# Hybrid decoder layer on one core: the routing stage works by sets of tiles with three-slot rings, and one raw buffer stays allocated across three stages

## The reference

```
mod = silu(c) @ w_ada + b_ada;  sh1, sc1, g1, sh2, sc2, g2 = split(mod, 6)
u   = x * (1 + sc1) + sh1
proj = u @ w_in                      # conv B | conv C | conv x | q | k | v | gate_A | gate_B
y_a = (B * dwconv3(C * xc)) @ w_a;   y_b = stick_breaking_attention(q, k, v) @ w_b
mix = (sigmoid(gA) * y_a + sigmoid(gB) * y_b) @ w_o
x   = layer_norm(alpha * x + g1 * mix)
u2  = x * (1 + sc2) + sh2
aff = sigmoid(u2 @ w_router)         # 16 experts in 4 groups
# best group by the sum of its top 2 of (aff + b_router), top 2 experts in it,
# gates = their aff over the sum; a token's row goes to both experts, in blocks of 128 rows
ffn = sum over both of gate * (silu(u2 @ w_gate[e]) * (u2 @ w_up[e])) @ w_down[e]
out = layer_norm(alpha * x + g2 * ffn)
```

## Time and profile before

| | us |
|---|---|
| median of three runs | 2847.39 (2843.78 to 2850.57) |
| the profiled execution | 2846.57 |
| its span, first to last instruction | 2844.0 |
| PE busy | 2526.8 (89%) |
| DVE busy | 1517.7 (53%) |
| ACT busy | 1118.3 (39%) |
| POOL busy | 866.5 (30%) |
| mean granted PE clock | 0.940 |
| one high part of 128x1024 on ACT (L1270) | 1.06 |
| one copy-out of u2, two halves, on ACT (L1285) | 1.08 |
| one sum of two products of a unit on POOL (L1060) | 1.28 |
| one turn of a tile's u2 on PE up to the next instruction (L1238) | 0.87 |

### The profile page before, as it was taken

How to read it: one execution, slowest core, us unless ns; L and a number is a source line. 1 busy time by engine, 2 the same in 40 slices (tenths; PEclk the granted TensorE clock), 3 DMA queues, 4 the chain that set the end, 5 groups by cost and what they waited for, 6 DMA issues and landing times. The chain is left out here.

```text
span 2844.0 us, 37196 instructions
## 1 busy us (share of the span) xinstructions
PE 2526.8 (89%) x12564; PEld 2105.7 (74%) x12565; DVE 1517.7 (53%) x2156; ACT 1118.3 (39%) x1817; POOL 866.5 (30%) x755
## 2 busy tenths in 40 slices
PE   4999799899999999999969969993998999999970
PEld 3888677778888888888857747883787888888750
DVE  4211165666565666566632248985556544526636
ACT  2211154554454545454520012220556545536633
POOL 1111044442222222222301225664222222322236
PEclk7999899999999999999989989995999999999985
DMA  6655687767666575646455554343667656636735
GB/s 236 246 188 184 187 266 223 233 211 221 200 202 195 196 219 167 205 153 200 147 193 168 160 189 134 126 133 113 210 192 228 205 149 180 204 91 198 259 74 236
DMA packets 252442, 534.86 MB, mean 188 GB/s; under 512 B 23156, under 2 KB 92904, under 8 KB 250664
## 3 DMA queue, kind: packets, MB, share of 16 engines
q1 hardware_dynamic: 229736, 468.39, 50.1%
q0 software_dynamic: 15248, 46.62, 7.7%
q10 hardware_dynamic: 7344, 18.35, 1.7%
HBM read 380.26 MB, written 153.02 MB: 188 GB/s over the span
## 5 line engine op out<-in xcount | busy, mean ns | idle before, releaser
L89 PE MATMUL mx_acc<-u_u,mx_w_hi 128*128 128x512 f32 x1792 | 572.7, 401 | 2.1 <-DMA mx_w_lo<-halves 2.1
L608 POOL TENSOR_TENSOR mx_wt<-mx_wt,mx_rest 128x127 f32<-128x127 f32 (+15 forms) x128 | 271.4, 2120 | 701.1 <-DVE mx_rest L813 701.1
L89 PEld LDWEIGHTS mx_acc<-u_u,mx_w_hi 128*128 128x128 f32 x1792 | 326.8, 190 | 66.5 <-DMA mx_w_lo<-halves 2.5
L821 DVE TENSOR_TENSOR mx_wt_lo<-mx_p_t,mx_wt_hi 128x512 fp32r<-128x512 f32 (+2 forms) x320 | 192.1, 604 | 332.5 <-ACT mx_wt_hi L774 330.4
L89 PE MATMUL mx_acc<-u_u,mx_w_lo 128*128 128x512 f32 x896 | 354.2, 395 | 0.0
L774 ACT ACTIVATE mx_wt_hi<-mx_p_t 128x512 fp32r<-128x512 f32 (+2 forms) x320 | 170.5, 533 | 400.4 <-PE mx_p_t L662 353.5
L813 DVE TENSOR_TENSOR_SCAN mx_rest<-mx_rest,mx_zero 128x128 f32<-128x128 f32 (+15 forms) x128 | 319.4, 2496 | 13.5 <-ACT mx_wt L756 13.5
L89 PE MATMUL moe_p_gu<-moe_gu_hi,moe_x_hi 128*128 128x512 f32 x656 | 263.0, 401 | 16.4 <-DVE moe_gu_lo L1773 16.4
L89 PE MATMUL moe_p_gu<-moe_gu_hi,moe_x_lo 128*128 128x512 f32 x656 | 259.2, 395 | 0.0
L89 PE MATMUL moe_p_gu<-moe_gu_lo,moe_x_hi 128*128 128x512 f32 x656 | 258.8, 395 | 0.0
L662 PE MATMUL mx_p_t<-keep_ident,mx_wt 128*128 128x128 f32 x1088 | 174.9, 276 | 37.4 <-POOL mx_wt L608 28.9
(11 more groups left out here) (244 smaller groups left out, 5262.8 us busy)
## 6 DMA issues: line engine op xcount, KB each, us to landing
mx_w_hi<-halves SPq DMA_DIRECT2D x84, 512.0 KB, 4.0
mx_w_lo<-halves SPq DMA_DIRECT2D x84, 512.0 KB, 5.5
moe_gu_raw<-in_w_gate SPq DMA_DIRECT2D x64, 512.0 KB, 5.7
moe_gu_raw<-in_w_up SPq DMA_DIRECT2D x64, 512.0 KB, 6.7
moe_dn_raw<-in_w_down SPq DMA_DIRECT2D x32, 1024.0 KB, 6.9
u_saved<-u_u SPq DMA_DIRECT2D x4, 4096.0 KB, 16.8
mx_w_mod<-in_w_ada SPq DMA_DIRECT2D x64, 256.0 KB, 5.2
gate_t<-mx_g_out SPq DMA_DIRECT2D x64, 256.0 KB, 5.1
```

The costliest lines, as they stand in the source:

```text
L89: mm = pe.matmul(out, a, b, start=first and n == 0, stop=last and n == len(pairs) - 1, skip_group_check=True)
L608: pool.tensor_tensor(wt[:, t % 2, 0:w - 1], wt[:, t % 2, 0:w - 1], rest[:, t % 2, 1:w], ALU.mult).then_inc(m["weights_done"], 1)
L821: dve.tensor_tensor(wt_lo[:, first:first + k - j], p_t[:, n % TR, 0:(k - j) * P].rearrange("p (j t) -> p j t", t=P), f32(wt_hi[:, first:fi ...
```

## The change

It has five parts.

1. `front`: the ring has four slots (RS = 4) of half the width (MH = MW // 2). w_ada comes in 16 halves of 0.5 MB; x is asked for behind all of them; the 32 column sums are PE's first work, ahead of the four turns. The q, k, v weights come in 16 pieces of half the columns: first the 8 pieces with columns 0 to 767 (units 0 to 5), then the 8 others; PE waits for all of them ahead of unit 6.
2. A buffer `stay` of two parts of 32 KB in each partition is allocated once, ahead of `branch_outputs`, and kept through `experts`. All raw tiles of the three stages are views of it, and the semaphores `ahead` live as long.
3. `branch_outputs`: DVE writes its products into `prod` (two slots) rather than over the gates, and waits for the store of two units ago; a gate slot is refilled when DVE has multiplied it. Behind the gate loads of the first token block SP loads all of w_o into the first part of `stay`.
4. `mix_norm_route` is written out for 16 tiles without a loop. g1 is multiplied into w_o (8 DVE instructions at the start) rather than into each tile, and alpha * x + mix is one DVE instruction for each half tile, straight from PSUM. At the start PE works on tiles 0 and 1 side by side as the parts of w_o are split. `a_hi`, `a_lo` and `u2` have three slots. DVE's order in a step is norm of t, u2 of t, low part of t+3, then put and choose where they fall. Routing is done for sets of tiles (0-3, 4-7, 8-11, 12-13, 14-15) with DVE instructions that cover the set: choose in steps 5, 9, 13, 16, 17, put in steps 7, 11, 15, 17, 18. PE's turn stands behind the second of the eight parts of the products, router products and rank behind the sixth. The table of block rows is computed with one row in each partition and turned by PE.
5. The six pieces of the first expert's weights are loaded in steps 1 to 6 of that stage; `experts` starts with the split, and turns to the gathered rows after it.

```diff
-        ring = s.sb("ring", [P, 2, MW])
+        ring = s.sb("ring", [P, RS, MH])
...
+            for n in range(2 * KD):
+                k, half = divmod(n, 2)
+
+                past(sp, m["summed"], n - RS + 1)
+                sp.dma_start(ring[:, n % RS], ada_view[:, k, half * MH:(half + 1) * MH]).then_inc(ring_in[n % RS], 16)
+            sp.dma_start(xr[:], x_view[:, 0]).then_inc(m["x_in"], 16)
...
+                    if tb == 0 and i == WH // P:
+                        pe.wait_ge(m["w_lo_done"], 2 * KD)
...
-                sp.wait_ge(stored[d % RB], 16 * (tb * (KD // RB) + d // RB + 1))
+                sp.wait_ge(m["prod_done"], 2 * (tb * KD + d) + 2)
                 sp.dma_start(gates[:, d % RB], gate_v[d * P:(d + 1) * P, :, bass.ds(tb * NB, NB)]
...
             rest_of(0)
+            for k in range(KD):
+
+                sp.wait_ge(m["w_lo_done"], k * WQ // KD + 1)
+                sp.dma_start(flat(stay, 0)[:, k * D:(k + 1) * D], w_o.rearrange("l (k p) n -> (l p) k n", p=P)[:, k]
+                             ).then_inc(ahead["w_o"][k], 16)
...
+                    dve.wait_ge(stored[d % 2], 16 * (tb * (KD // 2) + d // 2 + 1))
                     for n in range(2):
-                        dve.tensor_tensor(gates[:, d % RB, n], acc[:, d % RB, n], gates[:, d % RB, n], ALU.mult
+                        dve.tensor_tensor(prod[:, d % 2, n], acc[:, d % RB, n], gates[:, d % RB, n], ALU.mult
...
+    SETS = ((0, 4), (4, 8), (8, 12), (12, 14), (14, 16))
+    AR, UR = 3, 3
+    CHOOSE_AT = {5: 0, 9: 1, 13: 2, 16: 3, 17: 4}
+    RANK_AT = {7: 0, 11: 1, 15: 2, 17: 3, 18: 4}
...
+            for t in range(2, STEPS):
+                if t < NT:
+                    pe.wait_ge(m["a_lo_done"], t + 1)
+                    pe.wait_ge(m["mix_used"], 2 * t - 2)
                     for k in range(KD):
+                        mix(t, k)
+                        if k == 1:
+                            turn(t - 2)
+                        if k == 5:
+                            logits(t - 2)
+                        if k == 5 and t in RANK_AT:
+                            rank(RANK_AT[t])
...
+            for t in range(STEPS):
+                if t < NT:
+                    rows_out(t - 2)
...
+                    act.wait_ge(m["rstd_done"], t + 1)
+                    past(act, x1_stored[t % 2], 16 * (t // 2))
+                    act.activation(x1t[:, t % 2], y[:], ACT.Identity, bias=offset[:], scale=rstd[:]
                                    ).then_inc(m["normed"], 1)
+                if t + 3 < NT:
+                    high(t + 3)
+                if t < NT - 1:
+                    affinities(t - 2)
...
+                for n in range(2):
+                    w = slice(n * NB, (n + 1) * NB)
+                    dve.scalar_tensor_tensor(out=y[:, w], in0=xt[:, t % 2, w], scalar=ALPHA, in1=p_mix[:, t % 2, n],
+                                             op0=ALU.mult, op1=ALU.add).then_inc(m["mix_used"], 1)
...
-            high_x(0)
             split_gu(0, None)
+            high_x(0)
```

More of the change, by code:

```diff
@@ L231, in part @@
                     mm.then_inc(m["pe_done"], 1)
+            for j in range(FIRST_COLS):
+                half, a = divmod(j * P, MH)
+                if a == 0:
+                    pe.wait_ge(m["summed"], 2 * KD - 1 + half)
+                mm = pe.matmul(p_mod[:, j:j + 1], msum[:, half, a:a + P], one[:], start=True, stop=True,
+                               skip_group_check=True)
+            mm.then_inc(m["mod_summed"], 1)
             for k in range(TR):
                 turn(0, k)
[L235 to L239, removed]
             pe.wait_ge(m["cols_out"], 2)
@@ L1053, in _ @@
         def _(pool):
-            for i in range(RB):
+            for i in range(2):
                 pool.sem_inc(stored[i], 16)
@@ L1059, in _ @@
                     pool.wait_ge(m["prod_done"], 2 * u + 2 + 2 * RB)
[L1060 removed]
+                    pool.tensor_tensor(prod[:, d % 2, 0], prod[:, d % 2, 0], prod[:, d % 2, 1], ALU.add
                                        ).then_inc(m["sum_done"], 1)
[L1064 to L1086 removed]
 class Chain:
@@ L1151, in mix_norm_route @@
         m = {n: s.sem(n) for n in names}
-        w_in = [s.sem(f"w_in{i}") for i in range(WR)]
+        w_in = ahead["w_o"]
         a_in = [s.sem(f"a_in{i}") for i in range(2)]
@@ L1272, in _ @@
[L1272 to L1283 removed]
+                act.wait_ge(a_in[t % 2], 16 * (t // 2) + 16)
@@ L1382, in _ @@
[L1382 to L1396 removed]
+                dve.wait_ge(m["a_hi_done"], t + 1)
@@ L1482, in step @@
+            dve.wait_ge(m["const_done"], 1)
+            low(2)
+            for t in range(STEPS):
+                if t < NT:
                     norm(t)
-                if isinstance(t.i, int) and t.i == 0 and t.o == 0:
+                if t == 0:
                     second_rows()
-                if (t + -2).live:
-                    choose(t + -2)
-                if (t + -3).live:
-                    put(t + -3)
-                if t.live:
-                    affine(t)
-            pipeline(dve, step, 3)
@@ L1515, in _ @@
-            ch.link(dve.tensor_reduce(moved[:], begun[:], AX.X, ALU.max))
-            dve.scalar_tensor_tensor(out=block_row[:], in0=number[:], scalar=float(P), in1=moved[:], op0=ALU.mult,
-                                     op1=ALU.add)
-def experts(nc, used, keep, w_gate, w_up, w_down, mod_rows, ln2_g, ln2_b, u2_rows, records, acc, ln_g, ln_b):
+                if t < NT:
+                    affine(t)
+                if t + 3 < NT:
+                    low(t + 3)
+                if t in RANK_AT:
+                    put(RANK_AT[t])
@@ new lines, in _ @@
+            tail.link(dve.tensor_tensor(begun[:], number[:].to_broadcast([P, E]), n_rows[:], ALU.is_ge))
+            tail.link(dve.tensor_tensor(begun[:], begun[:], shift[:], ALU.mult))
+            tail.link(dve.tensor_reduce(moved[:], begun[:], AX.X, ALU.max))
+            dve.scalar_tensor_tensor(out=row[:], in0=number[:], scalar=float(P), in1=moved[:], op0=ALU.mult,
+                                     op1=ALU.add).then_inc(m["rows_known"], 1)
+            dve.wait_ge(m["rows_turned"], 1)
@@ L1542, in experts @@
         m = {n: s.sem(n) for n in names}
-        piece_in = [s.sem(f"piece_in{i}") for i in range(PIECES)]
+        piece_in = ahead["piece"]
         block = ctx.enter_context(nc.Block())
@@ L1948, in hybrid_layer @@
         }
+        ahead = {"w_o": [s.sem(f"w_o{k}") for k in range(KD)], "piece": [s.sem(f"piece{i}") for i in range(PIECES)]}
         with ExitStack() as uctx:
```

727 lines of the change are left out of this document (380 added, 347 removed).

## The result

The changed kernel takes **2827.95 us** (median of 4 runs, 2825.41 to 2830.37); the kernel before, beside it, 2846.41. The ratio is 0.9941, with a 95% interval of 0.9928 to 0.9953. The direction was right. The size was not: 18 us came where 45 were forecast, and 2828 lies above the range of 2783 to 2821. The profiled execution has a span of 2827.1 us, against 2844.0.

A forecast was written before the change was run, and what follows sets the result against it. PE was taken to bound nearly all of the program, with DVE pacing the routing stage. Gains of 14 (front), 9 (branch), 19 (routing) and 3 (experts), 45 in all, took 2846.6 to 2801.6, stated as 2801; range 2783 to 2821.

The forecast's parts named there:

- Front, 14 forecast: Front: half-width pieces and earlier column sums bring PE's products forward; gain 14 us, bounds 7 and 16.
- The second half of the weights has two units, 11 us, of cover: Front: two units of PE work, 11 us, cover the arrival of the second half of the weights.
- The eight steps: Front: the eight contraction steps of the first four units take 25.5 us instead of 30.1, 4.6 gained.
- Branch stage, 9 forecast: Branch stage: both PE waits for DVE's products, 9.4 us together, go; gain 9 us, bounds 4 and 9.4.
- the load goes out 7 us earlier and DVE is there at 1522.4: Branch stage: earlier token load brings DVE to the next block's gates at 1522.4, not 1529.38, before PE fills four accumulators.
- 7.0 us for two units: Branch stage: product, sum, issue and store landing of 4.1 take DVE 7.0 us per two units, against PE's 10.9.
- The rival with the two slots: Branch stage: DVE's store waits pace PE once landings pass 8 us; at 12, total 2874; chance 5% with the like.
- have 20 us before they are needed: Branch stage: gates queued on SP behind the eight w_o loads still have 20 us before they are needed.
- Routing stage and experts' start, 23 forecast: Routing stage gains 19 us, bounds 5 and 30; experts' start gains 3, bounds 0 and 8.
- The three waits of 7 us: Routing stage: each set at 5, 9 and 13 makes PE's router products wait 7 us for ACT's copy.
- 3 x 1.23: Routing start: DVE does low part, scaling and low part from 1659.20, so PE starts at 1662.9.
- the clock: Routing stage: rival where the clock falls in each tile, PE needing 1.6 more in most; 12 us, 2814; chance 14%.

The follow-up runs named there:

- the run that takes both waits away: Changed kernel with front's first save of u in four pieces behind the first four stores and the last two weight pieces split after two units leave: 2819.2 us.

## Why the prediction was wrong

**Front, 14 forecast, about 4 measured.** Two terms failed. The first product came at 42.19 and not 38.3, because the sixteen pieces came more slowly than 1.25 to 1.5 us each: DVE's last addition ends at 31.8, 25.5 us after its first instruction began, 1.6 each, and after that first one DVE stood waiting for a piece nine times. The queues were full (DMA share 0.97) but moved 335 GB/s in that stretch, not the 419 that the forecast took from the earlier trace rows. The step that cost more is the sentence "The second half of the weights has two units, 11 us, of cover". It counted what PE needs and not what else stands in the same order: units 0 to 3 are evicted behind all sixteen pieces on ACT and DVE, and their stores are queued behind the 6 MB that front had asked for before. That is 5.9 us of PE's waits, and 2 to 3 of lower clock; the run that takes both waits away is 8.8 us faster. The eight steps came out somewhat better than forecast: 23.5 us from the first product to the end of the fourth unit, for 25.5.

**Branch stage, 9 forecast, -3 measured.** The step that failed is "the load goes out 7 us earlier and DVE is there at 1522.4". The stretch counted was that from unit 7 on, with DVE taken to be at PE's heels. The catching up in front of it was not counted: DVE is behind by up to four units at each block's start, and two slots let it regain one pair in 8.9 us rather than four units in 4.9. The sum "7.0 us for two units" used a landing of 4.1 and measured 8.9, since the landing is 5.7. The 7.0 was compared with PE's 10.9 in steady state, where it does not matter, and not with the 4.9 of the catching up. The date 1522.4 stands on the scale of the kernel before and is 65.0 us after the stage's first product; before it was 72.0, and the changed kernel has 75.5. With four slots it is 69.0: the load goes out 5.3 us earlier in the stage rather than 7, and takes 1.5 to 2 us longer to land (9.7 and 12.4). Half of the 7 was enough, since the stage is then 11 us shorter than before, for the 9. The rival with the two slots named the right mechanism and the wrong point of decision: it took the pace of the whole stage, at a landing of 8, for what decides. What decides is the late load, and at 5.7 the gain is lost already. That the gates behind w_o "have 20 us before they are needed" was no answer either: it left out the stores. From 1474 to 1526 us they land in 6.8 us with w_o in the queues and 6.0 without it, and with products in place in 6.2 for 4.1. This is the likely way, not shown by itself, in which w_o costs 4 and 3 us of waiting.

**Routing stage and experts' start, 23 forecast, 16.3 measured** from the first product on. PE's 13.75 a tile (13.65), the choose step of 22.2 (21.2), POOL's hold on the first of its instructions (2.42), the unheld norm from PSUM (1.28) and the held low part (3.4) all came, and the last norm to the tables took 27.1 for 29. The three waits of 7 us measure 5.9, 6.0 and 3.9. Four terms were mis-sized. One is the lower clock behind each wait, put at 1.6: four tiles with a set cost 65.3 less 4 x 13.65, 10.7 us, of which 5.9 are the wait and 4.8 are left for the clock. It is 0.50 in 1782 to 1787, the router products take 3.59 there where they take 1.85 in other tiles, and it is 0.56 in 1787 to 1792. So a set cost 10.7 and not 8.6. The next is the start: the third norm comes 51.0 us after the first product, for 47.5, PE waiting 5.8 for the first turned rows. The first product itself came 16.5 us after the branch stage's last, for 15.4 forecast: DVE begins when it should (1657.41), but "3 x 1.23" left out that the second piece is scaled ahead of the first one's low part, so there are four instructions. The last link is 2.3 longer than taken from before: POOL's sixteen scatters stand at the end in a row, 1.26 us each, end 1.7 us behind the last of DVE's work, and the next stage starts 7.2 us after them for 4.9. Of the rivals, the clock did not come as told: in a tile without a set it is 1.00 (1740.42 to 1754.04), and in the stretches read here it falls only behind PE's waits.

**The bounds.** The lower ends, 7 for front and 4 for the branch stage, left no room for a wait that the change itself adds, and in both stages it did. Added up, the bounds allowed a gain of 16 us and 18 came; the range of the total, which ends at 2821, was cut closer than its own bounds.

## What to carry over

When a buffer loses slots, look for the place where its engine has fallen behind, and price the catching up there; then ask which load or eviction stands behind the last unit in program order. An order that gives an engine less to wait for does nothing if the accumulators are emptied behind the same list. And a request that needs only a free buffer should be placed where the buffer comes free, not at the end of the loop body: that one move was worth 14 us here, and shortened the stage by 16.6 us where four slots gave 14.2.

## What the runs showed of the hardware

A 256 KB store of the branch stage landed later in most kernels in which the next 512 KB gate load is asked for ahead of it or beside it. The median from issue to landing is 4.1 us in the kernel before and 3.6 in the run with products in place, where the load follows the store. It is 5.4 to 6.0 in the changed kernel and ten of its variants, one of them without w_o in the queues, and 4.6 in the last, which has the tokens early and no w_o. The last has the same order of load and store as the ten, so the order is not all of it, and nothing here changes it alone: the cause is argued, not shown.

POOL holds DVE's type casts too, and not only instructions with two inputs. In the tail of the routing stage, with POOL's multiply from 1926.92 to 1929.53:

```profile
1927.55 0.29 DVE L1558 TENSOR_REDUCE mix_dest_f<-mix_picked 128x8 f32<-128x128 f32 x1
1927.87 1.69 DVE L1560 CAST mix_dest<-mix_dest_f 128x8 uint32<-128x8 f32 x1
1929.47 0.18 DVE L1504 TENSOR_TENSOR mix_sel<-mix_aff,mix_br 128x32 f32<-128x32 f32 x1
```

The cast of eight elements takes 1.69 us, and 0.17 to 0.20 when POOL is not at such work; the reduction just ahead of it is not held. In front six of the eight casts of u shown up to 56 us take 1.52 us, until about 0.3 us after POOL's subtraction ends (such as 43.22 to 44.74, with POOL's end at 44.45), and 0.41 to 0.43 otherwise. The Trainium skill (SBUF — State Buffer, Who interferes with whom) names copies and casts as instructions that can take both of DVE's ports and then contend with GpSimd, and the reduction as one that does not; the trace agrees, and the prediction had used only the page's rule on two inputs.
